# A two-layer block on one core: the first normalised inputs are made tile by tile, as their modulation weights arrive

## The reference, cut to what matters

```
mod = silu(c) @ ada_w + ada_b                    # 6 x 1024 values: shift, scale, gate, ...
sh1, sc1, g1, sh2, sc2, g2 = split(mod, 6)
csh1, csc1, ... = split(silu(c_ctx) @ ada_w + ada_b, 6)
rms_norm(x, g) = x * rsqrt(mean(x*x, features) + 1e-6) * g
hc = rms_norm(ctx, norm1_g) * (1 + csc1) + csh1  # 256 context tokens
hx = rms_norm(x, norm1_g) * (1 + sc1) + sh1      # 1024 tokens
cb, cc, cx, r, k, v, w_lo, a_lo, g_lo = split(h @ w_in)
```

## Time and profile before

| | us |
|---|---|
| median of 3 runs | 2268.68 |
| lowest and highest of them | 2260.36, 2268.76 |
| span of the profiled execution | 2265.7 |
| last transfer of ada used by TensorE | 41.61 |
| first token-group h_lo used by TensorE | 58.49 |
| first product of v | 81.94 |
| TensorE busy over the span | 2050.2 (90%) |
| VectorE, ScalarE, GpSimd busy | 1500.4, 892.1, 773.6 |

### The profile page before, as it was taken

One profiled execution on the slowest core, in us unless ns is written; L12 is line 12 of the kernel. 1 busy time (PEld: TensorE's weight loads), 2 busy tenths in 40 slices (PEclk: granted clock), 3 DMA queues, 4 the chain that ended last, 5 costly groups with the idle time before them and its releaser, 6 DMA issues. The chain is left out here.

```text
span 2265.7 us, 37012 instructions
## 1 busy us (share of the span) xinstructions
PE 2050.2 (90%) x15072; PEld 1594.0 (70%) x15072; DVE 1500.4 (66%) x2052; ACT 892.1 (39%) x1445; POOL 773.6 (34%) x460
## 2 busy tenths in 40 slices
PE   4989999837878898999999979999899999999898
PEld 1767677636767676788877768887677776776566
DVE  5777767679774548788988870454746676546644
ACT  5453443414434637333333331443434354333320
POOL 1144433300030145877777724533321111111111
PEclk7999999958899999999999999999999999999899
DMA  7535444597655422122221274523211111102512
GB/s 308 182 122 174 151 141 130 154 264 197 167 177 143 159 75 75 56 84 84 84 76 73 84 272 139 177 73 122 85 56 56 66 38 47 66 19 84 195 47 84
DMA packets 181335, 271.16 MB, mean 120 GB/s; under 512 B 74280, under 2 KB 122024, under 8 KB 176816
## 3 DMA queue, kind: packets, MB, share of 16 engines
q1 hardware_dynamic: 164816, 250.57, 33.9%
q10 hardware_dynamic: 16352, 18.22, 2.7%
HBM read 200.53 MB, written 68.23 MB: 119 GB/s over the span
## 5 line engine op out<-in xcount | busy, mean ns | idle before, releaser
L105 PE MATMUL b_ps<-h_hi,b_wpool 128*128 128x512 f32 (+1 forms) x896 | 277.4, 387 | 10.8 <-POOL b_wpool L744 10.8
L2995 PE MATMUL g_ps<-g_h_hi,w 128*128 128x512 f32 x784 | 260.0, 403 | 6.0 <-ACT g_q L3192 5.9
L3313 POOL TENSOR_TENSOR w<-raw_down,w 128x1024 fp32r<-128x1024 f32 x38 | 94.5, 2488 | 464.6 <-ACT w L3168 464.6
L2262 DVE SCALAR_TENSOR_TENSOR e_vars<-grid,vec,e_vars 128x1024 f32<-128x1024 f32 x168 | 216.0, 1285 | 7.4 <-ACT e_vars L2009 4.2
L105 PEld LDWEIGHTS b_ps<-h_hi,b_wpool 128*128 128x128 f32 x896 | 167.8, 192 | 56.3 <-POOL b_wpool L744 14.4
L2995 PEld LDWEIGHTS g_ps<-g_h_hi,w 128*128 128x128 f32 x784 | 149.3, 190 | 40.8 <-ACT g_q L3192 6.9
L105 PE MATMUL b_ps<-h_lo,b_wpool 128*128 128x512 f32 (+1 forms) x448 | 170.6, 381 | 0.0
L2995 PE MATMUL g_ps<-g_h_lo,w 128*128 128x512 f32 x392 | 156.1, 398 | 0.0
L2674 POOL TENSOR_TENSOR g_down_lo<-raw_down,g_down_hi 128x1408 fp32r<-128x1408 f32 x26 | 86.7, 3339 | 142.5 <-ACT g_down_hi L2574 142.5
L2513 PE MATMUL g_pb<-g_z_hi,g_down_hi 128*128 128x512 f32 x286 | 114.8, 401 | 14.7 <-DVE g_down_lo L2751 9.8
L744 POOL TENSOR_TENSOR b_wpool<-raw_in,b_wpool 128x1024 fp32r<-128x1024 f32 x26 | 67.9, 2611 | 173.2 <-ACT b_wpool L530 173.2
(11 more groups left out here) (524 smaller groups left out, 5284.4 us busy)
## 6 DMA issues: line engine op xcount, KB each, us to landing
e_raw_up<-w_ffn SPq DMA_DIRECT2D x22, 1024.0 KB, 4.9
raw_down<-w_down SPq DMA_DIRECT2D x32, 704.0 KB, 4.2
c_op<-ops SPq DMA_DIRECT2D x40, 512.0 KB, 5.0
raw_down<-w SPq DMA_DIRECT2D x38, 512.0 KB, 3.7
raw_in<-w SPq DMA_DIRECT2D x26, 512.0 KB, 4.2
mod_stage<-ada_rows ACTq DMA_DIRECT2D x24, 512.0 KB, 3.7
zs<-e_z SPq DMA_DIRECT2D x21, 512.0 KB, 2.6
ops<-b_xin SPq DMA_DIRECT2D x20, 512.0 KB, 4.7
```

What stands on the lines that cost most here:

```text
L105: last = nc.tensor.matmul(out, w[:, k, :], x[:, k, cols], start=(k == 0 and n == 0), stop=(k == nk - 1 and n == 2))
L2262: STT(out=acc, in0=view, scalar=wt, in1=acc, op0=ALU.mult, op1=ALU.add).then_inc(sem("conv"), 1)
L2995: mm = nc.tensor.matmul(out_bank, ww[w % 2][:, k], xx[g][:, k], start=(k == 0 and a == 0), stop=(k == KD - 1 and a == 2))
L3313: nc.gpsimd.tensor_tensor(w_lo[w % 2], raw[:, w % 2], w_hi[w % 2].bitcast(F32), ALU.subtract).then_inc(sem("lo"), 1)
```

## The change

The prologue is reordered by feature tiles.

- The modulation weights are arranged so that one tile holds all 1024 input features for 128 shifts and 128 scales. Tile k alone then gives shift and gain of feature tile k. Each tile has its own place in memory, the raw g weight too (it goes into c_row), so among these SyncE waits for the eighth's place alone. TensorE's modulated(k) is sixteen instructions of 256 columns, picked(k) two small fp32 products.
- Tokens are loaded first, in four pieces, and squared and summed first; the context's squares, sums, root and inputs are put inside the loop. There is one exponential for both token groups.
- One loop over kt on each engine: VectorE's input_pre(kt+1) makes gain times root times input over 1024 columns, in place, ScalarE's input_high(kt) adds the shift and rounds, VectorE's input_low(kt) adds the shift and subtracts. The context pieces follow two tiles behind (C_LAG). TensorE does w for both token groups at kt, g at kt - 3 (G_LAG), and the whole of w for the context behind the loop.
- Five modulation vectors are taken in the loop, at kt 3 to 7, and rows for them and the next are loaded there by ScalarE.

```diff
-    GADA = KD
     ROOT_SHIFT = 10
-    SLOTS_ADA = 3
-    K_DVE = K_ORDER = tuple(range(KD))
+    SEQ_COLS, CTX_COLS = slice(CTX, TOK), slice(0, CTX)
+    G_LAG, C_LAG, MOD_LAG = 3, 2, 3
+    MODS_IN_LOOP = KD - MOD_LAG
...
-    MODS_BY = {("w", 1): 6, ("w", 2): 8, ("v", 0): 10, ("v", 1): 12, ("v", 2): 14, ("k", 1): 15, ("k", 2): 16}
+    MODS_BY = {("w", 1): 10, ("w", 2): 11, ("g", 1): 12, ("w", 0): 13, ("v", 0): 14, ("k", 1): 15, ("k", 2): 16}
...
+    FIRST = [("w", 0, 1), ("w", 0, 2), ("g", 0, 1), ("g", 0, 2), ("w", 0, 0)]
+    CHUNKS = FIRST + [(x, 0, g) for x, g in V0_FIRST]
...
+            for g in (1, 2):
+                for part in range(2):
+                    rows = slice(4 * part, 4 * part + 4)
+                    sp.dma_start(xin[:, rows, cols(g)], d["xT"][:, rows, seq(g)]).then_inc(sem(f"x{g}{part}"), 16)
             load_ada(0)
+            load_w(("w", 0))
+            sp.dma_start(con, d["consts"][:, 0:NKEPT]).then_inc(sem("consts"), 16)
+            load_ada(1)
             sp.dma_start(xin[:, :, 0:CTX], d["ctxT"]).then_inc(sem("x0"), 16)
+            load_ada(2)
+            load_w(("g", 0))
+            for kt in range(3, KD):
+                load_ada(kt)
...
+            def modulated(k):
+                if k == 0:
+                    pe.wait_ge(sem("silu_c"), 1)
+                    pe.wait_ge(sem("rows_clear"), 2)
+                elif k >= 2:
+                    pe.wait_ge(sem("mod_rows"), k - 1)
+                pe.wait_ge(sem(f"ada_in{k}"), 16)
+                for half in range(2):
                     for b in range(4):
+                        i = 4 * half + b
+                        mm = nc.tensor.matmul(rowps[k % 2][32 * b:32 * b + 2], silu_c[:, i, :], ada_cols[k][:, i], start=half == 0,
+                                              stop=half == 1)
+                mm.then_inc(sem("ada_used"), 1)
+            def picked(k):
+                pe.wait_ge(sem("mod_rows"), k + 1)
+                if k == 0:
+                    pe.wait_ge(sem("row_sum"), 1)
+                elif k >= 2:
+                    pe.wait_ge(sem("gain"), k - 1)
+                for x in range(2):
+                    mm = nc.tensor.matmul(mod_cols[k % 2][:, x], mod_rows[k % 2][:, P * x:P * (x + 1)], row_sum[:], start=True, stop=True)
                 mm.then_inc(sem("mod_cols"), 1)
...
+            def first_dense(x, g, k):
+                pe.wait_ge(sem("h_lo") if g else sem("h_lo_c"), k + 1)
+                i = chunk[(x, 0, g)]
+                if k == 0:
                     pe.wait_ge(sem("lo"), tile_no[(x, 0)] + 1)
                     if i >= 4:
                         pe.wait_ge(sem("read_a"), act_read[CHUNKS[i - 4]])
+                    else:
+                        pe.wait_ge(sem("log"), 2 if x == "w" else 3)
+                w_hi, w_lo = weights(slot[(x, 0)])
+                out = ps[i % 4][:, 0:width(g)]
+                for n, (w, h) in enumerate(((w_hi, h_hi), (w_hi, h_lo), (w_lo, h_hi))):
+                    mm = nc.tensor.matmul(out, w[:, k, :], h[:, k, cols(g)], start=(k == 0 and n == 0), stop=(k == KD - 1 and n == 2))
+                if k == KD - 1:
+                    mm.then_inc(sem("chunk"), 1)
...
+            sums(0, 1)
+            modulated(0)
+            sums(1, 2)
+            picked(0)
+            modulated(1)
+            picked(1)
+            for kt in range(KD + G_LAG):
+                for g in (1, 2) if kt < KD else ():
+                    first_dense("w", g, kt)
+                if kt == 0:
+                    modulated(2)
+                if kt + 2 < KD:
+                    picked(kt + 2)
+                if kt == 1:
+                    sums(2, 0)
+                for g in (1, 2) if kt >= G_LAG else ():
+                    first_dense("g", g, kt - G_LAG)
+                if kt + 3 < KD:
+                    modulated(kt + 3)
+            for kt in range(KD):
+                first_dense("w", 0, kt)
...
+            def rows_kept(k):
+                act.wait_ge(sem("ada_used"), k + 1)
+                if k >= 2:
+                    act.wait_ge(sem("mod_cols"), k - 1)
+                A(mod_rows[k % 2], rowps[k % 2], ACT.Copy).then_inc(sem("mod_rows"), 1)
+            def gains(k):
+                act.wait_ge(sem("mod_cols"), k + 1)
+                if k == 0:
+                    act.wait_ge(sem("gain_of_bias"), 1)
+                A(t["mod"][:, :, k], mod_cols[k % 2][:, 0], ACT.Identity, bias=t["v_ada_b"][:, k:k + 1])
+                A(gain[:, :, k], mod_cols[k % 2][:, 1], ACT.Identity, scale=t["v_norm1_g"][:, k:k + 1],
+                  bias=gain_of_bias[:, k:k + 1]).then_inc(sem("gain"), 1)
+            def input_high(k):
+                act.wait_ge(sem("pre"), k + 1)
+                if k in (2, 4, 6):
+                    act.wait_ge(sem("ada_used"), {2: 3, 4: 4, 6: 6}[k])
+                A(h_hi[:, k, SEQ_COLS], xin[:, k, SEQ_COLS], ACT.Identity, bias=t["mod"][:, 0, k:k + 1]).then_inc(sem("h_hi"), 1)
+            def context_high(k):
+                act.wait_ge(sem("pre_c"), k + 1)
+                A(h_hi[:, k, CTX_COLS], xin[:, k, CTX_COLS], ACT.Identity, bias=t["mod"][:, 1, k:k + 1]).then_inc(sem("h_hi_c"), 1)
...
+            root_log(0, 1)
+            rows_kept(0)
+            root_log(1, 2)
+            act.wait_ge(sem("log"), 2)
+            A(rstd[:, SEQ_COLS], rstd[:, SEQ_COLS], ACT.Exp, scale=-0.5).then_inc(sem("rstd"), 1)
+            gains(0)
             hi("w", 0)
+            rows_kept(1)
+            for kt in range(KD + C_LAG):
+                if kt + 1 < KD:
+                    gains(kt + 1)
+                if kt < KD:
+                    input_high(kt)
+                if kt >= C_LAG:
+                    context_high(kt - C_LAG)
+                if kt + 2 < KD:
+                    rows_kept(kt + 2)
+                if kt == 0:
+                    squares(0, 0)
+                if kt == 1:
+                    root_log(2, 0)
+                    act.wait_ge(sem("log"), 3)
+                    A(rstd[:, CTX_COLS], rstd[:, CTX_COLS], ACT.Exp, scale=-0.5).then_inc(sem("rstd"), 1)
+                    hi("g", 0)
+                    act.wait_ge(sem("c_in"), 16)
+                    A(c_row, c_row, ACT.Silu).then_inc(sem("c_row"), 1)
+                if kt == 2:
+                    for i in range(5):
+                        load_mod(i)
+                if kt == 3:
+                    load_mod(5)
+                if kt == 4:
+                    hi("v", 0)
+                if 5 <= kt < KD:
+                    load_mod(kt + 1)
+            mods = KD + 1
...
+            def input_pre(k):
+                dve.wait_ge(sem("gain"), k + 1)
+                if k == 0:
+                    dve.wait_ge(sem("rstd"), 1)
+                STT(out=xin[:, k, SEQ_COLS], in0=xin[:, k, SEQ_COLS], scalar=gain[:, 0, k:k + 1], in1=rstd[:, SEQ_COLS], op0=ALU.mult,
+                    op1=ALU.mult).then_inc(sem("pre"), 1)
+            def input_low(k):
+                dve.wait_ge(sem("h_hi"), k + 1)
+                STT(out=h_lo[:, k, SEQ_COLS], in0=xin[:, k, SEQ_COLS], scalar=t["mod"][:, 0, k:k + 1],
+                    in1=h_hi[:, k, SEQ_COLS].bitcast(F32), op0=ALU.add, op1=ALU.subtract).then_inc(sem("h_lo"), 1)
...
+            folded(0, 1)
+            folded(1, 2)
+            dve.wait_ge(sem("consts"), 16)
+            nc.vector.tensor_reduce(row_sum[:], t["c_ident"].rearrange("p (b z) -> p z b", z=32)[:, 0:2], mybir.AxisListType.X,
+                                    ALU.add).then_inc(sem("row_sum"), 1)
+            input_pre(0)
+            for kt in range(KD + C_LAG):
+                if kt + 1 < KD:
+                    input_pre(kt + 1)
+                if kt >= C_LAG:
+                    context_pre(kt - C_LAG)
+                if kt < KD:
+                    input_low(kt)
+                if kt >= C_LAG:
+                    context_low(kt - C_LAG)
+                if kt == 0:
+                    folded(2, 0)
+                if kt == MOD_LAG:
+                    dve.wait_ge(sem("c_row"), 1)
+                if MOD_LAG <= kt < KD:
+                    modulation(kt - MOD_LAG)
...
-        "ada": a["ada_w"][0][:, 0:2 * D].reshape(KD, P, 2 * D),
+        "ada": a["ada_w"][0][:, 0:2 * D].reshape(KD, P, 2, KD, P).transpose(3, 1, 0, 2, 4).reshape(KD, P, 2 * D),
```

More of the change, by code:

```diff
@@ L642, in _ @@
-            hi("v", 0)
-            mods = 2
-            for x, g in (("w", 0), ("w", 1), ("g", 1), ("w", 2), ("g", 2)):
+            for g in (1, 2):
+                for part in range(2):
+                    squares(g, part)
+            act.wait_ge(sem("eps"), 2)
+            root_log(0, 1)
[4 more added lines that the diff above has]
+            gains(0)
@@ L645, in _ @@
+            mods = KD + 1
+            for x, _, g in FIRST:
                 src = there(x, 0, g)
@@ new lines, in context_pre, with context_low @@
+            def context_pre(k):
+                if k == 0:
+                    dve.wait_ge(sem("rstd"), 2)
```

(8 more changed lines are left out.)

220 lines of the change are left out of this document (76 added, 144 removed).

## The result

| | before | changed |
|---|---|---|
| median of runs, us | 2264.80 (4 runs, 2260.36 to 2268.76) | 2285.68 (4 runs, 2282.05 to 2288.66) |
| ratio with its 95% interval | | 1.0089 [1.0068, 1.0110] |
| span of the profiled execution, us | 2265.7 | 2282.2 |
| first product of v (T), us | 81.94 | 96.69 |
| granted clock, mean | 0.957 | 0.955 |

The changed kernel is slower by 0.9%; forecast were 2285 us and, with 64%, slower by over 0.5%. Of the 16.5 us between the two spans, 14.75 are there when TensorE starts on v (15.9 forecast).

What follows compares the result with a forecast made beforehand. Everything later was taken to hang on T, with VectorE gapless before it, making inputs. Start, first tiles, loop and tail gave T 97.8 against 81.94, 15.9 us more; 2268.7 + 15.9 = 2284.6, rounded 2285; range 2269 to 2294.

Steps and rivals of the forecast that it cites:

- the ring: Loop: low(k), w(k), picked(k+2), gains(k+2), pre(k+2), low(k+1) wait in turn; 5.65 us a turn, four turns 22.6.
- rival 1: Loop has slack, VectorE's occupation alone sets it: low(0) to low(7) under 38 us, 2261 to 2263; chance 7%.
- Up to the first lower half: Start: token landings, squares, sums, first gain at 27.8, then pre and low on VectorE; low(0) ends at 34.4 us.
- Rival 3: TensorE at the higher clock from the start: T 90.3, time 2277; chance 13%.
- low(1) and low(2): Second and third lower halves, behind queued TensorE, ScalarE and VectorE work: 11.6 and 14.8 us, ending at 46.0 and 60.8.
- Higher after low(2): TensorE's clock in the loop: lower level taken until low(2), the higher after it.
- Rival 2: Lower clock stays in the loop, a turn is TensorE's own 7.9 us: 2294 or more; chance 11%.
- 1 us for v: GpSimd's subtraction for v's lower half keeps VectorE out in the loop: 1 us, bounds 0 and 2.5.
- low(7) and the tail: Loop end: low(7) 3.6 us after low(6); then w(7), four g tiles and the context's w, 9.8 us to T.
- That move saves nothing: Five modulation vectors moved from behind T into the loop: no gain, since the keys had waited 2.35 us for ScalarE's copy.
- Behind T: After v starts: order kept, TensorE's 2.12 us idle left, the 7.07 us wait for GpSimd moves along with T.
- rival 4: Delay absorbed behind T as the 7.07 us or 2.12 us wait shrinks: 2270 to 2276; chance 9%.

Runs made afterwards that it cites:

- the pick ahead of w: Changed kernel with modulated(2) and picked(kt+2) ahead of w(kt) on TensorE; median 2267.31 us, 1.0019 of the kernel before, T 82.14.
- the spread: Changed kernel with ScalarE's high half of g, silu of the row and load_mod(5) moved to later turns; median 2278.15 us, ratio 1.0066 to the kernel before.
- the unused products: Changed kernel with eight more 256-column products, results unused, on TensorE at the end of kt 2 to 6; one run, 2273.23 us, T 94.92.
- the experiment: Changed kernel with the five modulation vectors, and the loads of rows 6 to 8, taken out of the loop to follow it; one run, 2284.2 us.
- The second pair of profiles: Changed kernel and kernel before, each profiled once more unaltered: T 96.01 and 81.09, spans 2273.1 and 2270.7 us; repeat ratio 1.0069.

## Why the prediction was right

**What bounds, and the ring.** Right, and shown by the pick ahead of w: one move on one queue took 14.55 us of T back, of 14.75, a part of it through the clock (above). "The queue orders in the diff", which spoke against rival 1, were indeed what decided: from the first lower half to the last the changed kernel took 55.4 us, forecast 53.6, needed for rival 1 under 38. With the pick, the sums, the modulations and the context moved it takes 31.7, which shows that rival 1's loop existed, for another order of the queues.

**Up to the first lower half: 34.4 forecast, 31.48 measured.** Landings held (squares at 7.13 and 15.73; 7.5 and 15.1 forecast). The step that failed is the clock of the first products. The sums of the second half were put at 3.78 and took 1.98; modulated(0) 1.08, not 1.89; the first gain came at 25.7, not 27.8. Rival 3 had this mechanism; its start is what happened, its steady loop is not. GpSimd's subtraction of w cost VectorE 0.46 (pre(1) took 1.74 instead of 1.28), where 1 was put; in the other kernels the same pre took 1.75 to 2.16.

**low(1) and low(2): 11.6 and 14.8 forecast, 11.10 and 13.28 measured.** Right in mechanism, with ScalarE's queue shown by the spread; 1.5 us of the second was too much. The sum took every price at the lower clock, and the clock was at 0.81 from 45 to 56: the context's sums took 1.11 and not 2.1.

**The ring's turns: 5.65 forecast, 7.08, 6.96, 6.58 and 7.02 measured, 27.64 for 22.6.** This is the term that was mis-sized, by 4.0 after the microsecond for v, which was counted apart. "Higher after low(2)" failed: at 76.5 to 79.8 the clock was 0.50, at 56 to 60 it was 0.58. At 1.00 the turns took 5.50 (the unused products). Rival 2 was therefore half true, on top of a start that was half rival 3; the errors (2.9 early, 0.5 and 1.5 early, 4.0 late, 0.3 early) nearly cancel and left T at 96.69 for 97.8. The Trainium skill (TensorE: Matmul & The Clock Gate, section HAM oscillation — how this bites in real kernels) describes a loop whose short bursts of matmuls each begin at the lower clock, because of the wait for a transfer before them. This trace agrees in part: in the turns the waits are for VectorE, 1.05 to 2.53 us, and the bursts at 62.99 and 76.54 begin at the lower clock (0.79 and 0.80 for the first product), but that at 69.96 doesn't (0.50, with the clock at 1.00 from 69.4 to 76.0).

**GpSimd and VectorE: 1 us for v.** In the changed kernel a subtraction of 3.14 us from 70.54 held a VectorE instruction of one column:

```profile
70.54 3.14 POOL L830 TENSOR_TENSOR b_wpool<-raw_in,b_wpool 128x1024 fp32r<-128x1024 f32 x1 [17.95 <-ACT b_wpool L575]
...
71.48 2.22 DVE L892 TENSOR_TENSOR mod<-b_acc,vec 128x1 f32<-128x1 f32 x1
```

It usually takes 0.16, so 2.06 are lost; the turn without a wait for the clock is longer by 1.07 (6.58 against 5.51 in the kernel with unused products). The 1 stands, and in a ring without slack it is 1.9 to 2.2 (6.77 against 4.5 to 4.9 with the pick ahead).

**low(7) and the tail.** 3.6 forecast, 3.33; tail 9.8, measured 9.86.

**"That move saves nothing".** For the loop it is shown that the vectors cost nothing except 1.35 in the last step. What they save behind T isn't measured, since the experiment also moved loads.

**Behind T.** Forecast was the order kept at a constant shift. TensorE's 2.12 us wait became 1.93; the other answers to the 7.07:

```profile
163.25 0.79 PE L105 MATMUL b_ps<-h_hi,b_wpool 128*128 128x512 f32 x1 [7.08 <-POOL b_wpool L830]
```

The wait is the same, 7.08, and the shift there 13.0: 1.8 us of the 14.75 are given back between 94 and 163. The clock did it, as far as the records show: the kernel before had a stretch at 0.84 which the changed one did not have at the same place in its work; ten microseconds at 0.84 are 1.6 short of ten at 1.00. The second pair of profiles agrees: the kernel before has 0.83 from 92 to 102, the changed one 1.00 from 107 to 119, and the shift falls from 14.9 to 13.3. First the kernel before, from 94 to 104, then the changed one:

```profile
94.00:104.00 10.00, 10.00 (x54) 0.84 0.81 291
```

```profile
107.00:119.00 12.00, 11.88 (x69) 1.00 0.26 85
```

That is rival 4's size only in part (for 2270 to 2276, 8.6 to 14.6 of the forecast's 15.9 us would have had to go), and not by its mechanism. Beyond 340 us the shift moves between about 8 and 16.8 us with no event to name, as it does between two executions of one kernel; that 16.5 stand at the end and not 13 is inside that scatter and was not explained further.

So the forecast of 2285 is right by its mechanism, with the clock's course wrong in both directions: too low at the start, too high in the ring. That the sum came so near is partly luck.

## What to carry to other kernels

Before changing what the engines do, write down, for each engine, its instructions in the order of the queue, and look for a circle: a short instruction that the next turn needs, queued behind a long one that waits for this turn. Moving it ahead adds no work and brought 14.5 us here, a part of it because the clock then stayed at 1.00; that engines had less to do in total brought nothing as long as the circle was closed. Then look at what the clock will be in a loop full of short waits, and at which pieces that were moved "behind" come last at the end, or stand in a queue ahead of something that another engine waits for.
